# Sixteen more gathered rows in flight from step to step, and a new interleaving of the expert rows with the mixer's work

## The reference

```
q = (xf @ w_q).reshape(t, PEER_HEADS, 2, PEER_DKEY // 2)
scores = einsum('thpd,hpnd->thpn', q, sub_keys)
s_top, i_top = top_k(scores, 16)
cand = s_top[:, :, 0, :, None] + s_top[:, :, 1, None, :]
best, pos = top_k(cand, 16);  gates = softmax(best)
hid = gelu(einsum('td,thkd->thk', x_blk, u_tab[idx_blk]))
coef = g_blk * hid
out = einsum('thk,thkd->td', coef, v_tab[idx_blk])
```

## Time and profile before

| | |
|---|---|
| median of three runs | 3565.8 us |
| time of the profiled execution | 3563.19 us |
| its span | 3561.5 us |
| VectorE busy | 2377.2 us (67%) |
| TensorE matmuls busy | 2114.5 us (59%), at a mean granted clock of 0.759 |
| GpSimd busy (the gathers) | 1990.8 us (56%) |
| ScalarE busy | 740.7 us (21%) |
| moved by DMA | 1291.01 MB, mean 362 GB/s |
| of it by the 2048 gathers | 1073.87 MB, 76.9% of the DMA engines' time |

### The profile page before, as it was taken

One profiled execution on the slowest core, in us unless ns is written; L12 is line 12 of the kernel. 1 busy time (PEld: TensorE's weight loads), 2 busy tenths in 40 slices (PEclk: granted clock), 3 DMA queues, 4 the chain that ended last, 5 costly groups with the idle time before them and its releaser, 6 DMA issues.

```text
span 3561.5 us, 33718 instructions
## 1 busy us (share of the span) xinstructions
PE 2114.5 (59%) x9182; PEld 982.8 (28%) x9182; DVE 2377.2 (67%) x5560; ACT 740.7 (21%) x1957; POOL 1990.8 (56%) x2067
## 2 busy tenths in 40 slices
PE   6672666577675456668675355668666274743235
PEld 3441342133431132234431132224422041300001
DVE  2519776776677886685777886685675986685540
ACT  2310221213212221212212221112222122110011
POOL 0003435655665757464665766465564775577675
PEclk8876877889777677789878587779868686875556
DMA  8244959999999989999999999999999998999999
GB/s 297 90 148 163 399 192 382 406 372 404 357 385 407 407 330 399 404 378 403 379 375 405 409 370 357 403 377 403 402 343 403 409 404 325 405 409 409 411 409 369
DMA packets 400241, 1291.01 MB, mean 362 GB/s; under 512 B 38110, under 2 KB 82660, under 8 KB 397868
## 3 DMA queue, kind: packets, MB, share of 16 engines
q0 software_dynamic: 294912, 1073.87, 76.9%
q1 hardware_dynamic: 97788, 183.35, 14.0%
q10 hardware_dynamic: 7344, 31.52, 2.2%
HBM read 1274.36 MB, written 14.23 MB: 362 GB/s over the span
## 4 chain that ended last, share of the span: by engine, by line
DMA 30%; DVE 26%; PE 22%; issue 10%; POOL 9%; ACT 3%; SPq 0%; DVEq 0%; POOLq 0%; ACTq 0%
DMA ring<-in_peer_v,idxR 15%; DMA ring<-in_peer_u,idxU 9%; PE work L761 9%; POOL ring L405 9%; DVE ring L1015 8%; PE work L734 4%; PE accs L748 4%; DMA wring<-in_w_in 3%; DMA wring<-in_peer_wq 3%; DVE proj L1027 2%; PE work L725 2%; DVE proj L1023 2%; ACT arena L446 2%; PE work L882 1%; PE work L873 1%
## 5 line engine op out<-in xcount | busy, mean ns | idle before, releaser
L1015 DVE CUSTOM_DVE_ANT_0 ring<-ring,n2U 128x1024 f32<-128x1024 f32 x1024 | 1213.4, 1219 | 396.0 <-DMA ring<-in_peer_u,idxU 378.0
L405 POOL DMA_INDIRECT ring<-in_peer_u,idxU x1024 | 986.7, 964 | 862.1 <-DVE idxU L1277 291.4
L405 POOL DMA_INDIRECT ring<-in_peer_v,idxR x1024 | 999.2, 976 | 689.1 <-PE accs L748 275.0
L748 PE MATMUL accs<-ring,wv 128*32 128x512 f32 x4096 | 723.8, 842 | 786.4 <-DMA ring<-in_peer_v,idxR 753.8
L761 PE MATMUL work<-wring,nT 128*128 128x512 f32 (+1 forms) x1408 | 672.2, 634 | 132.2 <-DMA wring<-in_peer_wq 81.3
L748 PEld LDWEIGHTS accs<-ring,wv 128*32 128x32 f32 x4096 | 149.3, 135 | 1281.1 <-issue 1134.9
L761 PEld LDWEIGHTS work<-wring,nT 128*128 128x128 f32 x1408 | 290.4, 212 | 504.8 <-issue 378.1
L467 ACT ACTIVATE wv<-stack,coefR 128x32 f32<-128x32 f32 x1024 | 237.8, 309 | 470.5 <-PE accs L748 403.2
L446 ACT ACTIVATE arena<-work 128x512 f32<-128x512 f32 (+1 forms) x214 | 120.2, 589 | 591.8 <-PE work L725 351.9
L446 ACT ACTIVATE proj<-work 128x512 f32<-128x512 f32 (+2 forms) x160 | 79.6, 508 | 671.2 <-PE work L761 594.2
L725 PE MATMUL work<-ident,proj 128*128 128x128 f32 x456 | 74.8, 315 | 175.8 <-DVE proj L1051 121.3
(11 more groups left out here) (216 smaller groups left out, 2052.6 us busy)
## 6 DMA issues: line engine op xcount, KB each, us to landing
wring<-in_w_in SPq DMA_DIRECT2D x80, 898.0 KB, 16.3
wring<-in_peer_wq SPq DMA_DIRECT2D x64, 1024.0 KB, 16.3
wring<-in_w_out SPq DMA_DIRECT2D x32, 1024.0 KB, 21.1
ring<-in_peer_u,idxU POOLq DMA_INDIRECT x1024, 12.1
ring<-in_peer_v,idxR POOLq DMA_INDIRECT x1024, 12.1
arena<-keys_scr ACTq DMA_DIRECT2D x8, 1024.0 KB, 8.2
proj<-proj_scr ACTq DMA_DIRECT2D x3, 1796.0 KB, 9.8
proj_scr<-n2A ACTq DMA_DIRECT2D x18, 224.5 KB, 7.1
```

The costliest lines, as they stand in the source:

```text
L405: nc.gpsimd.indirect_dma_start(ring[:, s * D:(s + 1) * D], None, table, bass.IndirectOffsetOnAxis(ap=idx, axis=0)).then_inc(row_in[s], 16)
L748: ins = nc.tensor.matmul(acc[c][quarter(r), :], wv[:, d * QUARTER:(d + 1) * QUARTER], ring[:, s * D + 512 * c:s * D + 512 * c + 512], star ...
L1015: V.tensor_tensor_reduce(out=rw, in0=rw, in1=n2U[:], scale=1.0, scalar=0.0, op0=ALU.mult, op1=ALU.add, accum_out=hid[:, kk:kk + 1]).then_i ...
```

## The change

`EARLY` goes from 4 to 8, so that a step ends with eight V of the second half instead of four, and all four plans are written anew. The number of U and V of steps 2 to 7 stays; step 1 has 24 V instead of 20 and step 8 has 40 instead of 44. No instruction is new and no operation has another shape. The diff in full:

```diff
-EARLY = 4
+EARLY = 8
...
-SELECT = "sc:G r0:V r1:V r2:CV r3:V r5:V r9:V r11:V r13:V r15:V r17:V r20:V r21:V"
+R8 = " ".join(f"r{i}:V" for i in range(11, 19))
 PLAN = {
-    "solo": "n0:LVVVVVVVVVVVV n1:UUU pj0:UUUUUU pj1:UUUUUU pj2:UUUUUU pj3:UUUUUU xT:U pj4:UUUU pj5:UUUU pj6:UUUU pj7:UUUUUUUUU conv:U cN:U kbT:U X0:U "
-            "L1:UUU L2:UU L3:UU L4:UU L5:UU L6:G vn:CS sn:HV y:V at1:UUUUUV at2:UUUUUV at3:UUUUUV pv3:UUUUUV op0:UUUUUUUUU op1:UUUUUU nm:U "
-            "wq0:UUUUUUU wq1:UUUUUUUV wq2:UUUUUUU wq3:UUUUUUUV " + SELECT,
-    "lead": "n0:L n1:UUUUUUUU pj0:UUUUUUU pj1:UUUUUUUV pj2:UUUUUUU pj3:UUUUUUUV xT:U pj4:UUUU pj5:UUUUV pj6:UUUUV pj7:UUUUUUUUU conv:V "
-            "cN:UV kbT:UV X0:V L1:UUUV L2:UV L3:UV L4:UGV L5:U L6:UUS vn:UUUUUC sn:HV y:V at1:UUUUUV at2:UUUUUV at3:UUUUUV pv3:UUUUU op0:UUUUUUUU op1:UUUUUV nm:U "
-            "wq0:UUUUUU wq1:UUUUUV wq2:UUUUU wq3:UUUUV " + SELECT,
-    "follow": "n0:LUUUUUUV pj0:UUUU pj1:UUUU pj2:UUUU pj3:UUUU xT:UUV pj4:UU pj5:UUV pj6:UU pj7:UUV conv:UUV cN:UUV kbT:UUV "
-              "X0:UUV L1:UUUV L2:UU L3:UUV L4:UU L5:UUV L6:UUU vn:UUUUUUU sn:UUUV y:GSH at1:CUUUU at2:UUUUUVV at3:UUUUUVV pv3:UUUUUVV op0:UUUUUUUUUV op1:UUUUUU nm:UU "
-              "wq0:UUUUUUU wq1:UUUUUUU wq2:UUUUUUU wq3:UUUUUUUV " + SELECT,
-    None: "end:L" + "UUUUUV" * 12 + "UUUUGUUUUSHUUUUC" + "UUUUV" * 14 + "GVVC" + "V" * NV}
+    "solo": "n0:LVVVVVVVV n1:UU pj0:UUUUUU pj1:UUUUUU pj2:UUUUUU pj3:UUUUUU xT:U pj4:UUUU pj5:UUUU pj6:UUUU pj7:UUUUUUU conv:U kbT:U X0:U "
+            "L1:UUU L2:U L3:U L4:U L5:U L6:UU vn:UUUUUUGS sn:H y:C at1:UUUUV at2:UUUUV at3:UUUUV pv3:UUUUUV op0:UUUUUUUUV op1:UUUUUV nm:U "
+            "wq0:UUUUUUUUUV wq1:UUUUUUUUV wq2:UUUUUUUUV wq3:UUUUUUUUV sc:G r0:V r1:C r2:V r4:V r5:V r7:V r9:V " + R8,
+    "lead": "n0:L n1:UUUUUUUU pj0:UUUUUUUV pj1:UUUUUUUUV pj2:UUUUUUUUV pj3:UUUUUUUUV xT:UU pj4:UUUUUUV pj5:UUUUUUV pj6:UUUUUUV pj7:UUUUUV conv:GSHUUUU "
+            "cN:C kbT:UV X0:UV L1:UV L2:UV L3:U L4:UUV L5:UV L6:UU vn:UUUUUU sn:V y:V at1:UUUUU at2:UUUUUV at3:UUUUUV pv3:UUUU op0:UUUUUUUU op1:UUUUU nm:U "
+            "wq0:UUUUV wq1:UUUUV wq2:UUV wq3:UV sc:G r0:V r1:C r5:V " + R8,
+    "follow": "n0:LUUUUUUUU pj0:UUUUUUV pj1:UUUUUUV pj2:UUUUUUV pj3:UUUUUUV xT:UU pj4:UUUU pj5:UUUUV pj6:UUUU pj7:UUUUV conv:UUUUV cN:UU kbT:UUUV "
+              "X0:SHUU L1:UUUG L3:CV L4:UUV L5:UUV L6:UU vn:UUUUUU sn:V y:UV at1:UUUUUV at2:UUUUUV at3:UUUUUV pv3:UUUUUV op0:UUUUUUUU op1:UUUUU nm:U "
+              "wq0:UUUUUV wq1:UUUUUV wq2:UUUUUV wq3:UUV sc:G r0:V r2:VC r5:V " + R8,
+    None: "end:L" + "UUUUUUUV" * 8 + "UUUUUUUUGUUUUSHUUUUC" + "UUUUV" * 14 + "GVVC" + "V" * NV}
```

## The result

The median is **3662.6 us** (four runs, 3654.8 to 3667.5) against 3566.2 us (four runs, 3563.2 to 3567.0) for the kernel before. The ratio is 1.027, with a 95% interval of 1.025 to 1.029. The forecast was 3538 us, so the change costs 96 us where 28 less were expected. The profiled execution has a span of 3662.1 us (before 3561.5).

The account below looks back on a forecast made before the run. It took full DMA (410 GB/s, 1.28 us a row) as the bound. Step 1 +7, three lead steps +5, three follow steps -9.7, step 8 -20.5 sum to -27.6, giving 3538 us; range 3485 to 3585, likeliest 3513 to 3558.

Parts of the forecast that it names:

- Step 8 by rows: Last step, 304 rows become 288 at 1.28 us each: -20.5 us, between -18 and -22.
- Vn to pv3: Mixers' stage where DMA leaks; H, C and a V leave its chain: -8 us a lead step, -14.7 a follow step.
- The selection: End of each step, from the first MAX8; length fixed by VectorE at 63.9 us, so change 0.
- The products of the follow step: Op0 to the selection, 47 rows for 53 and a fuller ring at its start: -16.7 us a follow step.
- "-8" for op0 to the selection: Lead step's products, 41 rows for 46 (-6.4) and a fuller ring (-1.6); TensorE busy 66 of 85.7 us, so room.
- Conv to L6: Lead step's stage after the front, 38 rows for 43, H and C coming in, a V leaving: +0.5 us.
- The front's "+20.5": Start of a lead step, 96 rows for 74: 28.2 us less 7.7 for six rows already in the ring.
- The stage is balanced ... By rows alone it would be 16 x 1.28 = 20.5: Follow step's n0 to L6 as one stage, 114 rows for 98, DMA full and VectorE busy 112 of 133 us: +21.7.
- the leak: Time in which DMA runs below 410 GB/s, 226 us in all; the follow step's dip in vn to pv3 was to close.
- Rival B: Lead front paid in full, products give nothing back because weights set the pace: lead step +19.7 us, 3582; chance 0.25.
- Rivals A and C: A: lead steps -7 us each, 3502, chance 0.18. C: step 1 eats step 8's gain, no change, 3567, chance 0.15.
- Step 1: Takes 16 rows from step 8: -12 us up to pv3, +19 in the products, +7 in all (-3 to +18).

## Why the prediction was wrong

**Where the 128 us between forecast and measurement lie.** Three lead steps 3 x (24.2 - 5) = 57.6, three follow steps 3 x (11.0 + 9.7) = 62.1, step 1 7.8, step 0 1.7, step 8 -1.1.

**Right.** Step 8 by rows: 373.2 us where 374 was said. Vn to pv3 in both kinds of step (-7.4 and -15.3 for -8 and -14.7). The selection stays at 63.8. The products of the follow step, -14.6 for -16.7.

**The step that failed in the lead steps** is the term "-8" for op0 to the selection, with its words "so there is room". TensorE's 66 busy us of 85.7 were read as room for the stage to shrink by 19 us. It did not: 85.6 us with 41 rows, 84.9 with 46. What the reading left out is the wait: two weight items of 24 us each, one behind the other, between TensorE's products. The chain of the kernel before shows them in steps 4 and 6. The runs show the bend near 48 rows: 101.2 us with 58, 100.1 with 57, 91.7 with 54, 85.2 with 49, 87.1 with 48, 85.6 with 46, 82.7 with 41, 84.0 with 36, and 77.3 with 33, where V had left. The 403 GB/s in that stage said that DMA was full; it did not say that nothing else would take as long. Conv to L6 is the same: 5 rows fewer, and with H and C in it +4.8 instead of +0.5. The front's "+20.5" was 28.2 less a credit of 7.7 for rows in the ring; measured +26.2, so most of that credit was not there. Of the 19.2 us by which a lead step was missed, op0 to the selection is 8.7, the front 5.7 and conv to L6 4.3.

**The step that failed in the follow steps** is "The stage is balanced ... By rows alone it would be 16 x 1.28 = 20.5". N0 to L6 is two stages. The front got 26 rows more and paid +38.1. Conv to L6 lost 10 rows and gave nothing, since S, H, G and C moved in and V16 behind C holds the ring there (87 GB/s for 22 us). Setting off the 10 against the 26 before pricing was the error. By rows the front would be 26 x 1.28 = 33.3, so 4.8 us of its 38.1 stay unexplained. The -14.7 of vn to pv3 was right, but the leak it closed opened one stage earlier.

**Rival B** was the nearest. Its mechanism (front paid in full, products give nothing back) and its deciding point, a lead step longer by over 14 us, are what the trace and the runs with dots moved show; its +19.7 a lead was +24.2. Its reason was that weights set the pace, and the trace bears that out: the chain of the stage goes through two weight items of 24 us in all three lead steps, and half rows, at the same TensorE work, make the stage 15 us shorter, so that work alone is not its floor. No run changes the weights' loads alone, so how much shorter the stage could be without that wait isn't shown. B still had follow steps at -9.7, so its 3582 fell short. Rivals A and C fall with the lead steps at +24.2 and follow steps at +11.0.

**Step 1** is +14.8 for +7. Its products took +23.0 for the +19 forecast, and conv to L6 +5.8. The rest of its forecast (-12 up to pv3) came to -4.5 - 9.5 + 5.8 = -8.2. Its last V, at r18, hold up the meeting, which falls into the front of step 2 and makes it +29.5 where steps 4 and 6 are +25.3 and +23.9: timeline of VectorE, kernel after,

```profile
747.67 0.69 DVE L1042 COPY proj<-hbuf 128x1024 f32 x1 [6.54 <-PEq L965]
```

**What is shown and what is not.** Shown: `EARLY` alone costs 0.3% under the conditions of the experiments; the lead plan carries most; V in its front charge 1.34 us a row and conv to L6 gives back a third; ten dots of the lead step cost 1.25% or nothing measurable, by how many rows the products hold; the products of the lead step wait for two weight items one after the other. Open: 0.4 to 0.6% of the loss is in no single part; the reading of the follow steps rests on the trace, as no run moves S, H, G and C alone; why six rows cost the lead front 11 us when they are dots; whether a gather's turn is DMA's 1.28 us or GpSimd's 1.24.

As a simple account by rows: in a lead step 22 rows went to the front, and 18 of them came out of stages that did not get shorter (5, 5 and 8). 18 x 1.28 = 23.0 us, against +24.2 measured. The sum agrees better than its parts do: conv to L6 became 4.8 us longer, and vn to pv3 7.4 shorter.

## What to carry to other kernels

A full transfer system in a stage means that rows added there cost; it does not mean that rows removed give back. Before moving work out of a stage, look at what the chain of work that ended last goes through there, in every step of the kind and not in one. Where it goes through something other than the rows, here the loads of the weights, the stage holds its rows free of charge, and moving them is paid where they go. The busy time of an engine doesn't show this floor: TensorE was busy 66 us of 85.7, and the waits between its products made up the rest. Price each stage by itself: do not set off fewer rows in one against more in the next, and where a dip closes, ask where the waiting chain went.

## What the runs showed of the hardware

**The same kernel under two conditions.** The kernel before ran at 3566 us in one place and at 3844 to 3900 in others. The rate inside step 8 differs. Windows, first the kernel after in the profile of its result:

```profile
3320.00:3600.00 280.00, 90.33 (x424) 17.61 (x428) 141.06 (x265) 26.34 (x107) 204.51 (x220) 0.55 1.03 410
```

then the kernel before in the experiments, inside step 8, and its step 3 from op0 to the selection:

```profile
3450.00:3800.00 350.00, 115.03 (x560) 23.46 (x560) 131.96 (x251) 35.38 (x147) 226.60 (x242) 0.63 0.96 368
...
1434.10:1536.70 102.60, 64.85 (x186) 28.95 (x179) 58.32 (x96) 10.38 (x24) 60.66 (x64) 0.82 1.03 402
```

The Trainium skill (HBM Reference, Specifications (TRN2)) says that two cores share one domain's bandwidth, with about 425 GB/s for a core alone and about 358 for each when both stream. The 410 here lies near the first. By that page the ceiling of 358 GB/s that the prediction weighed is the shared one. The 368 here should not be taken for it: DMA moved 402 GB/s in the same profile, and with half the bytes step 8 took as long, at 189 GB/s. What makes these chips slower isn't shown, nor what the neighbouring core did.

**A gather's issue is nearly as dear as its bytes.** With half the bytes GpSimd's mean for the gather of a U was 980 ns, with all of them 964 in the profile before; one follows the other after 0.30 us in both. The kernel gained 2%.

**A turn of the loop costs some 6 us.** The program is a loop over two steps, whose later turns begin with steps 4 and 6. At their start, in both kernels, VectorE stands still for 6.5 to 7.0 us, for nothing that the profile names; at the start of steps 2, 3 and 5 of the kernel before it was 0.7, 0.5 and 1.8 us. Timeline of VectorE, kernel after:

```profile
1598.99 0.69 DVE L1042 COPY proj<-hbuf 128x1024 f32 x1 [6.85 <-issue]
```
